# Reordering the first block of a two-block transformer kernel: convolution projection first, taps accumulated in PSUM, attention head by head beside half of the output projection

## What is computed

```python
h = rms_norm(x, mix_norm_g)
q, kv, gate_logits, conv_in = split(h @ w_in)        # 1024, 1536, 48 and 2048 columns
attn = nsa_attention(q, kv, sigmoid(gate_logits), rel_bias, ...)
# 16 query heads of 64, 4 key/value heads; per head three masked softmaxes
# (compressed blocks, selected blocks, window), each weighted with its gate
a, g = split(conv_in, 2)
u = causal_depthwise_conv(a * sigmoid(g), conv_w, conv_b)   # 31 taps, 1024 channels
conv = silu(layer_norm(u, conv_ln_g, conv_ln_b))
x = x + concatenate([attn, conv]) @ w_out            # 2048 x 2048
```

## Time and profile before

| | us |
|---|---|
| median of the runs | 3291.95 |
| profiled execution, its own time | 3304.61 |
| its span | 3302.8 |
| TensorE busy | 3011.6 (91%) |
| VectorE busy | 2169.6 (66%) |
| ScalarE busy | 1317.7 (40%) |
| mean granted TensorE clock | 0.953 of 2.4 GHz |

### The profile page before, as it was taken

How to read it: one execution, slowest core, us unless ns; L and a number is a source line. 1 busy time by engine, 2 the same in 40 slices (tenths; PEclk the granted TensorE clock), 3 DMA queues, 4 the chain that set the end, 5 groups by cost and what they waited for, 6 DMA issues and landing times.

```text
span 3302.8 us, 50584 instructions
## 1 busy us (share of the span) xinstructions
PE 3011.6 (91%) x16768; PEld 2582.1 (78%) x16768; DVE 2169.6 (66%) x3195; ACT 1317.7 (40%) x1706; POOL 2.2 (0%) x10
## 2 busy tenths in 40 slices
PE   4988767899999999977999998988998999999998
PEld 4867656788888888766878787777887888888887
DVE  4548885688578668556776565655765665665665
ACT  2324433444333333433444344444434443343332
POOL 0000000000000000000000000000000000000000
PEclk7987778999999999988999999999999999999999
DMA  8622214455555555533445454554554655555553
GB/s 172 190 66 64 77 51 132 124 191 175 194 176 180 188 168 186 170 104 95 143 142 166 153 162 131 153 151 134 190 186 128 194 185 186 185 184 188 187 168 125
DMA packets 587655, 507.08 MB, mean 154 GB/s; under 512 B 90027, under 2 KB 586427, under 8 KB 586939
## 3 DMA queue, kind: packets, MB, share of 16 engines
q1 hardware_dynamic: 577216, 501.42, 49.3%
q10 hardware_dynamic: 9803, 2.59, 0.6%
q0 software_dynamic: 560, 2.12, 0.2%
HBM read 503.88 MB, written 2.12 MB: 153 GB/s over the span
## 4 chain that ended last, share of the span: by engine, by line
PE 75%; DVE 16%; issue 4%; ACT 3%; DVEq 1%; SPq 1%; ACTq 0%; DMA 0%
PE banks L1279 46%; PE banks L1280 23%; DVE w_lo L767 4%; DVE arena L783 3%; DVE arena L989 2%; PE banks L1327 1%; ACT w_hi L508 1%; DVE arena L1045 1%; DVE arena L830 1%; PE banks L1266 1%; PE banks L1319 1%; DVE arena L817 1%; SPq L361 0%; DVE arena L1073 0%; DVE yp L1077 0%
## 5 line engine op out<-in xcount | busy, mean ns | idle before, releaser
L1279 PE MATMUL banks<-hp,w_hi 128*128 128x512 f32 x5120 | 1853.1, 406 | 118.3 <-DVE w_lo L767 74.0
L767 DVE TENSOR_TENSOR w_lo<-w_raw,w_hi 128x1024 fp32r<-128x1024 f32 (+2 forms) x960 | 1136.2, 1207 | 654.2 <-ACT w_hi L508 633.4
L508 ACT ACTIVATE w_hi<-w_raw 128x1024 fp32r<-128x1024 f32 (+2 forms) x960 | 989.4, 1044 | 1252.1 <-PE banks L1280 1070.0
L1280 PE MATMUL banks<-hp,w_lo 128*128 128x256 f32 x5120 | 1453.5, 284 | 0.0
L1279 PEld LDWEIGHTS banks<-hp,w_hi 128*128 128x128 f32 x5120 | 980.8, 192 | 373.4 <-issue 65.7
L1280 PEld LDWEIGHTS banks<-hp,w_lo 128*128 128x128 f32 x5120 | 986.4, 193 | 0.4
L1279 PE MATMUL banks<-yp,w_hi 128*128 128x512 f32 x2176 | 775.5, 401 | 27.5 <-DVE yp L1011 17.7
L1280 PE MATMUL banks<-yp,w_lo 128*128 128x256 f32 x2176 | 614.3, 282 | 0.0
L1279 PEld LDWEIGHTS banks<-yp,w_hi 128*128 128x128 f32 x2176 | 412.0, 189 | 130.7 <-DVE yp L1011 18.1
L1280 PEld LDWEIGHTS banks<-yp,w_lo 128*128 128x128 f32 x2176 | 414.8, 191 | 0.1
L783 DVE TENSOR_REDUCE arena<-banks 128x256 f32<-128x512 f32 (+1 forms) x392 | 251.0, 682 | 168.2 <-PE banks L1280 168.2
(11 more groups left out here) (195 smaller groups left out, 1422.3 us busy)
## 6 DMA issues: line engine op xcount, KB each, us to landing
w_raw<-in_w_in SPq DMA_DIRECT2D x480, 256.0 KB, 3.1
w_raw<-in_w_up SPq DMA_DIRECT2D x352, 256.0 KB, 3.4
w_raw<-in_w_ffn_up SPq DMA_DIRECT2D x176, 256.0 KB, 3.5
w_raw<-in_w_ffn_gate SPq DMA_DIRECT2D x176, 256.0 KB, 2.9
w_raw<-in_w_down SPq DMA_DIRECT2D x160, 256.0 KB, 2.9
w_raw<-in_w_ffn_down SPq DMA_DIRECT2D x160, 256.0 KB, 2.8
w_raw<-in_w_out SPq DMA_DIRECT2D x128, 256.0 KB, 3.2
w_raw<-in_w_mla_proj SPq DMA_DIRECT2D x64, 256.0 KB, 2.9
```

Of the source, the lines that this page charges most:

```text
L508: nc.scalar.activation(w_hi[:, s, 0:n], w_raw[:, s, 0:n], ACT.Copy).then_inc(hi_ready, 1)
L767: v.tensor_tensor(w_lo[:, s, 0:n], w_raw[:, s, 0:n], w_hi[:, s, 0:n].bitcast(f32), ALU.subtract)\
L1279: mm(banks[:, b, :], w_hi[:, s, at:at + P], rhs[:, kt, :], start=kt == 0, stop=False)
L1280: ins = mm(banks[:, b, 0:T], w_lo[:, s, at:at + P], rhs[:, kt, 0:T], start=False, stop=kt == kt_last)
```

## The change

The first block's phases are put in another order and written out without loops; the totals of units stay.

- Squares of x come before the first roundings. The convolution projection runs first (32 units, tile by tile, banks 0 to 3 in turn, one bias flip behind each tile), then keys and values (24), gates, q (16).
- The gate products of all tiles are kept (`u`, eight tiles). The taps are spread under the projections, 8 or 7 tap pairs in each group of four units, two tiles at a time, accumulated in bank 7. The last tap writes to SBUF.
- Sigmoids are ScalarE's own function instead of exponential, add and reciprocal.
- The compression runs between the groups of keys and values.
- Attention goes by single heads with three sets of banks and buffers: scores(h), then transposes and values of h-1. The scale of q is applied with the bias. VectorE multiplies by the weights instead of ScalarE.
- The conv half of w_out (its lower 1024 rows) becomes 16 units, each with all eight 128 x 128 pieces of one output tile, beside heads 6 to 15; the attention half stays a phase of four steps with 16 units.
- Low parts are formed on VectorE, as before. The buffers of the attention lie in the space of `hp`, the bias windows and compression tables in that of `yp`.

The core of the diff (SyncE's loads follow the new order of units; the second block is not touched):

```diff
-PHASES = [("q", 8, 2, 4), ("kv", 8, 3, 4), ("gates", 2, 1, 1)]
-PHASES += [(f"conv{g}", 4, GRP, 2) for g in range(2)]
-PHASES += [("w_out", 8, 4, 4)]
+UNIT0 = 6
+CONV_BANK = {11: 4, 12: 5, 14: 6, 15: 7}
+PHASES = [("conv", 32, 1, 16), ("kv", 24, 1, 12), ("gates", 2, 1, 1), ("q", 16, 1, 8), ("w_out_conv", 16, 1, 16),
+          ("w_out", 4, 4, 4)]
...
 # ScalarE
-            first("q")
-            norm(0)
+            x_squares("x_transposed", 1)
+            his("conv", 0, 0, 2)
+            norm(0, lambda b: hi("conv", 0, 2 + b))
...
+            for h in range(NQ):
+                if h >= 3 and h % 2:
+                    y_hi((h - 3) // 2)
+                exps(h)
...
+                if h >= 1:
+                    turned(h - 1)
...
+                if h >= UNIT0:
+                    hi("w_out_conv", 0, h - UNIT0 + 4)
...
 # VectorE
+            def taps(n0, n1):
+                for n in range(n0, n1):
+                    pr, k = divmod(n, TAPS)
+                    for a in range(2):
+                        t = 2 * pr + a
+                        acc, src, w = banks[:, 7, a * T:(a + 1) * T], u[:, t, k + 2:k + 2 + T], vcol("conv_w", t + k * CT)
+                        if k == 0:
+                            ins = v.tensor_scalar(acc, src, w, vcol("conv_b", t), ALU.mult, ALU.add)
+                        else:
+                            ins = v.scalar_tensor_tensor(conv_y[:, t, :] if k == TAPS - 1 else acc, src, w, acc, ALU.mult, ALU.add)
+                    link(ins)
...
+            for t in range(CT):
+                ph, j = ("conv", 4 * t + 4) if t + 1 < CT else ("kv", 0)
+                lows(ph, 0, j, j + 2)
+                if t >= 2:
+                    taps(8 * t - 16, 8 * t - 12)
+                lows(ph, 0, j + 2, j + 3)
+                used("conv", 0, 4 * t + 4)
+                take(glu[:, t % 2, 0, :], t % 2 * 2)
+                take(glu[:, t % 2, 1, :], t % 2 * 2 + 1)
+                lows(ph, 0, j + 3, j + 4)
+                if t >= 2:
+                    taps(8 * t - 12, 8 * t - 8)
+                flipped(t)
+                dve.wait_ge(sem("glu_sigmoid"), t + 1)
+                link(v.tensor_tensor(u[:, t, 32:], glu[:, t % 2, 0, :], glu[:, t % 2, 1, :], ALU.mult))
...
+            def weighted(h):
...
+                for j, (lo_, hi_) in enumerate(NSA_SEG):
+                    ins = v.tensor_scalar(e[:, lo_:hi_], e[:, lo_:hi_], c[:, j:j + 1], None, ALU.mult)
+                ins.then_inc(sem("nsa_p"), 1)
...
+            def conv_out(n):
+                used("w_out_conv", 0, n + 1)
+                b = CONV_BANK.get(n, 0)
+                link(v.tensor_tensor(x[:, n, :], banks[:, b, 0:T], x[:, n, :], ALU.add))
+                v.tensor_tensor(x[:, n, :], banks[:, b, T:], x[:, n, :], ALU.add).then_inc(chunk_out, 1)
...
+            for h in range(NQ):
+                scores(h)
+                if h >= 3 and h % 2:
+                    y_lo((h - 3) // 2)
...
+                if h >= 1:
+                    weighted(h - 1)
...
+                if h >= UNIT0 + 1:
+                    lo("w_out_conv", 0, h - UNIT0 + 3)
+                    conv_out(h - UNIT0 - 1)
...
 # TensorE
+            def conv_unit(n):
+                if n in (11, 12):
+                    pe.wait_ge(sem("nsa_pt"), NQ - 2)
+                elif n in (14, 15):
+                    pe.wait_ge(sem("nsa_pt"), NQ - 1)
+                else:
+                    free("w_out_conv", 0, min(n, 11))
+                unit("w_out_conv", 0, n, CT, 8, P, (CONV_BANK.get(n, 0),), yp, KT - 1, (sem("mixed"), 1), CT)
...
+            for h in range(NQ):
+                scores(h)
+                if h == 0:
+                    pe.wait_ge(sem("conv_done"), 1)
+                    sums(banks[:, 0, 0:T], conv_y, CT).then_inc(sem("conv_sum"), 1)
+                if h >= UNIT0:
+                    conv_unit(h - UNIT0)
+                if h >= 1:
+                    turns(h - 1)
+                    values(h - 1)
+                if h == 1:
+                    pe.wait_ge(sem("conv_squares"), 1)
+                    sums(banks[:, 0, T:], conv_sq, CT).then_inc(sem("conv_sum"), 1)
+            for n in range(10, 13):
+                conv_unit(n)
+            turns(NQ - 1)
+            conv_unit(13)
+            values(NQ - 1)
+            conv_unit(14)
+            conv_unit(15)
+            pe.wait_ge(sem("nsa_lo"), NQ // 2)
+            gemm("w_out", yp, CT, lambda u: None, 1)
```

More of the change, by code:

```diff
@@ L383, in _ @@
             w_in = A["w_in"][0]
[L386 to L389, removed]
-                        unit("q", i, 4 * g + u, [(lambda s, par=par, c=c: w_raw[:, s, 0:4 * GC].rearrange(
-                            "p (k c a d) -> p k c a d", k=4, c=2, a=2)[:, :, c, par, :],
-                            rows(w_in, 4 * u, 4, ds(cols[par], P))[:, :, c * HD:(c + 1) * HD])
-                            for par in range(2) for c in range(2)])
@@ L394, in _ @@
-            gemm("kv", w_in, 0, KT, KV0)
+            for t in range(CT):
+                for u in range(4):
+                    unit("conv", 0, 4 * t + u, [(lambda s, h=h: w_raw[:, s, 0:4 * GC].rearrange(
+                        "p (k n) -> p k n", n=GC)[:, :, h * P:(h + 1) * P],
+                        rows(w_in, 4 * u, 4, ds(CONV0 + h * CCH + t * P, P))) for h in range(2)])
+            for g in range(6):
+                for u in range(4):
+                    halves("kv", 0, 4 * g + u, w_in, 4 * u, 4, KV0 + g * GC)
@@ L650, in _ @@
+            his("w_out_conv", 0, 14, 16)
+            turned(NQ - 1)
+            y_hi(NQ // 2 - 1)
+            first("w_out")
             stream("w_out", post=squares("w_out"))
@@ L679, in _ @@
             first("mla")
-            def his(ph, i, j0, j1):
-                for j in range(j0, j1):
-                    hi(ph, i, j)
             def gate_sigmoid(ph, i, k0, dst):
@@ L1013, in residual @@
+            lo("w_out_conv", 0, 13)
+            conv_out(9)
+            lo("w_out_conv", 0, 14)
+            weighted(NQ - 1)
+            conv_out(10)
+            lo("w_out_conv", 0, 15)
+            for n in range(11, 14):
+                conv_out(n)
+            y_lo(7)
+            first("w_out")
+            conv_out(14)
+            conv_out(15)
             def residual(c0):
@@ new lines, in _ @@
+            pe.wait_ge(sem("v_tok"), 1)
+            for u in range(2):
+                unit("gates", 0, u, 8 * u, 8, P, (4,), hp, KT - 1)
+            for g in range(4):
+                free("q", 0, 2 * g - (2 if g >= 2 else 3))
+                for u in range(4):
+                    unit("q", 0, 4 * g + u, 4 * u, 4, GC, (g % 2 * 2, g % 2 * 2 + 1), hp, KT - 1)
+                if g == 0:
+                    free("gates", 0, 1)
+                    v_turn(2)
+                    for b in range(QB):
+                        ins = turn(banks[:, 6, 64 + b * NBR * NQ:64 + (b + 1) * NBR * NQ], g_sb[0:NBR * NQ, b * P:(b + 1) * P], NBR * NQ)
+                    ins.then_inc(sem("gates_turned"), 1)
@@ L1450, in _ @@
[L1450 to L1461 removed]
+            pe.wait_ge(sem("gates_tok"), 1)
```

632 lines of the change are left out of this document (310 added, 322 removed).

## The result

The changed kernel takes 3350.36 us, the median of four runs (3333.59 to 3355.02), against 3291.11 (3289.81 to 3291.95) beside it: 1.0153 times the time before, 95% interval 1.0117 to 1.0189. This ratio and those further down are the comparisons' own estimates; the quotient of the two medians, here 1.0180, is a little off it but inside the interval. The forecast was 3331, with 3290 to 3366 as its range.

The account below looks back on a forecast made before the run. VectorE was to pace the projections and chains of waits the heads: 323 + 92 + 148 + 35 + 50 = 648 against 608.3, so 3291.95 + 39.7 = 3331.6; forecast 3331 us, range 3290 to 3366.

Parts of the forecast that it names:

- Start: Block's start: sums can begin 20.5 us in because ScalarE's first copies stand behind the squares; everything behind 14 us earlier.
- restart: TensorE's start of unit 4, held up by ScalarE's twelve DMA issues; forecast to move from 72.3 to 58.3.
- The issues: ScalarE's twelve DMA issues at the start, taken as the same ones, 14.4 us with no copy, holding up unit 4.
- Projections: Convolution, keys and values, gates, q: VectorE sets the pace, 14.4 us a tile with taps; conv_done at 323.
- PSUM: Taps' accumulator written in PSUM: 0 to 0.13 us more a pair, 0 to 17 us in all; taken as 0.
- That rival (0.17): Taps in the projections: writing PSUM makes a pair 1.05 instead of 0.92, +17 us, 3348; chance 0.17.
- Heads 0 to 5: Attention heads without conv units: 27 for heads 0 and 1, 57 for 2 to 5, layer norm 8: 92 us.
- the ring: Heads below 6: scores, VectorE, transposes, ScalarE's copies, values, next scores as a closed chain at 1.2 GHz, 14.0 us a head.
- Late heads: From head 7 each unit waits for VectorE's add of the unit before, 6.65 us idle; 17.0 us a head.
- The clock rivals: Heads: clock stays at 2.4 GHz, 38 less, 3293, chance 0.10; or never rises, 36 more, 3367, chance 0.08.
- The faster rival: Heads overlap because the add of unit n-1 is never late: 10.3 to 11 us a head, 3268; chance 0.10.
- The sum: Block total 323 + 92 + 148 + 35 + 50 = 648 against 608.3: +39.7, added to the median 3291.95.

Follow-up runs that it names:

- The filler: Changed kernel plus eight useless TensorE products between scores and transposes in heads 3, 4 and 5: one run, 3343.96 us; last product at 646.9 instead of 652.9.
- both ways of taking it away: Changed kernel with VectorE's add ahead of the next head's scores, 3288.05 us, or with units alternating between banks 0 and 6, 3292.28 us.
- the earlier add: Changed kernel with VectorE adding unit n-1 into x ahead of the next head's scores: median 3288.05 us, 0.9968 of the kernel before.

## Why the prediction was right, and where it was off

The forecast, 3331, was 19 us short of the median and inside its range, and the mechanism that it named is the one that the experiments show.

- **Start.** First unit forecast at 36, measured 35.7; restart forecast at 58.3, measured 60.0. The issues take 14.8 us instead of 12.6: the step that took them over unchanged was 2 us short, and 5 in the kernel before with its squares first (17.7).
- **Projections.** `conv_done` forecast at 323, measured 325.8. The sum is VectorE's, and in VectorE's time it held step by step. Its six passes with taps took 14.2 us each (forecast 14.4) and ended at 167.1 (164), three groups of keys and values at 207.8 (206), the rest of them with the gates at 274.5 (272). Its waits there were 4.8 for the hidden layer, 4.5 and 5.4 for roundings and 8.1 for the gate units, 23 in all where I had 5, 5, 4 and 5; its work was 43 instead of 47, so part of this hit is luck. The largest miss is at the head: the first pass with taps began at 82.1, not 77, since VectorE waited 9.7 us for the first two sigmoids of ScalarE, for which the sum has no term (and its own terms, 58.3 + 2.3 + 4 x 2.78, give 72 and not 77). TensorE's own starts are other ones, because VectorE forms low parts a tile or a group ahead: its tiles 2 and 3 still went at 12.0, and its keys and values began at 154.3.
- **PSUM.** Taken at 0 with a bound of 17. The other taps cost 4 ns more than in SBUF, the first tap of a tile, a plain multiplication, 132 ns more: 232 x 4 ns and 8 x 132 ns are 2.0 us for all, and `conv_done` moved by 1.1, which is within the scatter. To go by the row with the same operation was right; the upper bound came from a multiplication that reads a bank (67 ns more), and one that writes a bank is dearer still, but there are few of them. The Trainium skill (Perfetto Trace Analysis, Optimizing Scalar/DVE Operations) would give 65 ns for either, as an estimate from its 60 and 125; the traces agree with it for neither, though they do for the multiplication that reads a bank (67). That rival (0.17) is closed.
- **Heads 0 to 5.** 92 forecast, 90.6 measured; heads 4 and 5 took 14.6 and 14.9 at 0.50, the ring's 14.0 to 14.2. The filler shows that the clock is in it: 5.2 us for a rise from 0.53 to 0.76.
- **Late heads.** 17.0 forecast, 17.0 measured; the gap 6.65 forecast, 6.0 to 6.3 measured; the unit behind it 4.5, measured 4.75. The cause was named (bank 0, the add last in VectorE's list) and both ways of taking it away confirm it. 148 forecast for heads 6 to 14, 148.3 measured; 35 for what follows, 38.1; 50 for w_out's other half, 50.3.
- **The clock rivals.** Neither extreme came: in a late head the clock is 0.50 for the first 4 us of the unit and 1.00 for transposes, values and scores, as the 17.0 assumed. What I did not see is that the clock follows the wait: without it heads were at 0.93 to 0.98 by themselves.
- **The faster rival.** It needed 10.3 to 11 us a head and gave 3268. With the earlier add the heads are there (10.3 to 12.5), and the median is 3288: its mechanism is real in that kernel, and what kept it out of the changed one is the place of one line, as the prediction held against it.
- **The sum.** +39.7 forecast for the block, +44.8 measured: 2.8 in the projections, 3.1 at the end of the heads, 1.4 less in heads 0 to 5, the rest near zero. Of the 18.8 us between 3331.6 and 3350.4, 5.1 are these; the other 13.6 are not of the block: 5.6 lie in the trace's tail and 8.0 in where the two sets of runs lie against their profiled executions. The step that was off there is the first, that a difference in the trace can be added to the median as it is; the profiled execution of before lay 12.7 above its median, and I took that as harmless. That the miss stayed inside the range owes something to luck: the tail alone moves a single execution by some 15 us.

## What to carry to other kernels

When three engines work on one item in turn, write down for each the order of its list and ask what the next item's producer is waiting for: here the emptying of a bank stood last in a list whose owner was itself waiting, and moving it first was worth 58 us, staging the items two apart and draining before producing another 61. A gap on TensorE is paid twice, once as a wait and once as a low clock in the work behind it, so count both when you price its cure. Compare two traces at the last point that was edited before comparing their ends: behind it the same program differed by 16 us.

## What was not expected of the hardware

- Matmuls of one program, at full clock and with no wait, take 391 to 394 or 399 ns (512 columns) over hundreds of microseconds, the one with the short tail and the other with the long one, from execution to execution. What chooses between them stays open; it is neither the edit (the changed kernel alone showed both) nor the chip.
- VectorE's price for a write to PSUM depends on the operation: 4 ns for a scalar-tensor-tensor that also reads the bank, 132 for a tensor-scalar that doesn't.
- ScalarE's issue of the same twelve loads took 12.6 us when it began at 56.9, and 14.8 and 17.7 when it began at 42.3 and 42.5; single issues of `cmp_pos` took 1.2 to 4.7. GpSimd issued the same twelve in 8.5 us (43.2 to 51.7), 0.5 us for each of `cmp_pos`.
